# Three weight buffers at three places of a 128-byte frame, in a two-block transformer kernel

## The reference, cut to what matters

```
z = h @ w_in                                  # first block: mixer
merged = sum of gates[i] * (y_i @ w_branch[i]);  y = merged @ w_out
a, g = split(h @ w_up);  y = (gelu(conv(a)) * g) @ w_down
proj = x @ gla_w_in;     y = (o * silu(g)) @ gla_w_out      # GLA layer
kv = x @ w_kv; proj = x @ swa_w_in; y = (o * silu(g)) @ swa_w_out   # last layer
```

## Time and profile before

| | us |
|---|---|
| median of three runs | 746.49 |
| profiled execution, device time | 748.46 |
| its span, first to last instruction | 746.7 |
| PE busy | 721.3 |
| DVE busy | 522.7 |
| ACT busy | 395.9 |
| POOL busy | 106.3 |

### The profile page before, as it was taken

The page is one execution under the profiler, slowest core; times in us unless marked ns, Lnnn a source line. Parts: engine busy times, 40 slices in busy tenths (PEclk is TensorE's granted clock), DMA queues, the critical chain, the costliest instruction groups (busy, mean ns, idle before and its releaser), DMA issues.

```text
span 746.7 us, 14086 instructions
## 1 busy us (share of the span) xinstructions
PE 721.3 (97%) x5900; PEld 702.3 (94%) x5900; DVE 522.7 (70%) x763; ACT 395.9 (53%) x564; POOL 106.3 (14%) x90
## 2 busy tenths in 40 slices
PE   8899999998999999999999999999999999999995
PEld 6789899897898999999999989999999999999995
DVE  4879878876888777787777656936674456556665
ACT  4197454554364555445445347646555455556552
POOL 0040000000520200000001230000005265443000
PEclk9999999999999999999999999999999999999998
DMA  8995575566364355656565634534446544333101
GB/s 342 410 362 173 226 283 206 197 257 232 124 226 170 115 190 205 206 190 212 212 269 215 230 111 171 180 141 143 160 164 244 199 171 144 123 129 114 57 1 57
DMA packets 22265, 141.13 MB, mean 189 GB/s; under 512 B 2389, under 2 KB 3029, under 8 KB 6458
## 3 DMA queue, kind: packets, MB, share of 16 engines
q1 hardware_dynamic: 21626, 137.28, 50.7%
q0 software_dynamic: 576, 2.95, 1.0%
HBM read 139.17 MB, written 1.05 MB: 188 GB/s over the span
## 4 chain that ended last, share of the span: by engine, by line
PE 70%; DVE 12%; issue 6%; ACT 6%; DMA 4%; POOL 1%; SPq 0%; DVEq 0%; ACTq 0%
PE res L1593 20%; PE res L1594 20%; PE res L1595 20%; ACT wsplit L640 4%; DVE wsplit L1056 3%; DVE raw L1069 2%; PE pX L1796 2%; DMA shared<-in_w_ada 2%; DMA raw<-in_wts 1%; PE pS L1776 1%; DVE shared L1069 1%; DMA y<-in_w_ada 1%; ACT sq L655 1%; PE pS L1829 1%; PE pT L1786 1%
## 5 line engine op out<-in xcount | busy, mean ns | idle before, releaser
L1593 PE MATMUL res<-hs,wsplit 128*128 128x256 f32 (+1 forms) x1120 | 317.5, 283 | 3.2 <-DVE wsplit L1056 1.5
L1594 PE MATMUL res<-hs,wsplit 128*128 128x256 f32 (+1 forms) x1120 | 311.7, 278 | 0.0
L1595 PE MATMUL res<-hs,wsplit 128*128 128x256 f32 (+1 forms) x1120 | 311.5, 278 | 0.0
L1056 DVE TENSOR_TENSOR wsplit<-raw,wsplit 128x2048 fp32r<-128x2048 f32 (+3 forms) x101 | 226.7, 2248 | 117.7 <-ACT wsplit L640 108.1
L640 ACT ACTIVATE wsplit<-raw 128x2048 fp32r<-128x2048 f32 (+3 forms) x101 | 188.2, 1865 | 104.3 <-issue 74.5
L1593 PEld LDWEIGHTS res<-hs,wsplit 128*128 128x128 f32 (+1 forms) x1120 | 209.3, 187 | 4.7 <-issue 2.3
L1594 PEld LDWEIGHTS res<-hs,wsplit 128*128 128x128 f32 (+1 forms) x1120 | 209.3, 187 | 0.4
L1595 PEld LDWEIGHTS res<-hs,wsplit 128*128 128x128 f32 (+1 forms) x1120 | 209.0, 187 | 0.2
L538 POOL TENSOR_TENSOR sq<-sq,rope 128x512 f32<-128x512 f32 x18 | 39.5, 2195 | 78.3 <-ACT sq L655 78.3
L1595 PE MATMUL res<-us,wsplit 128*128 128x256 f32 x176 | 48.6, 276 | 0.0
L1593 PE MATMUL res<-us,wsplit 128*128 128x256 f32 x176 | 48.6, 276 | 0.0
(11 more groups left out here) (336 smaller groups left out, 1213.8 us busy)
## 6 DMA issues: line engine op xcount, KB each, us to landing
raw<-in_wts SPq DMA_DIRECT2D x97, 1024.0 KB, 5.0
raw<-in_w_ada SPq DMA_DIRECT2D x16, 1024.0 KB, 5.4
shared<-in_w_ada SPq DMA_DIRECT2D x6, 1024.0 KB, 11.9
gates<-in_wts SPq DMA_DIRECT2D x4, 768.0 KB, 13.3
raw<-in_wts SPq DMA_DIRECT2D x4, 768.0 KB, 5.3
y<-in_w_ada SPq DMA_DIRECT2D x2, 1024.0 KB, 9.3
x<-in_xT SPq DMA_DIRECT2D x2, 512.0 KB, 4.5
gv<-in_ln_rows POOLq DMA_DIRECT2D x1, 1024.0 KB, 7.6
```

Of the source, the lines that this page charges most:

```text
L1056: nc.vector.tensor_tensor(halves(c)[:, 1, 0:b], raw[RAW_OF["w", c] % RAW][:, 0:b], halves(c)[:, 0, 0:b].bitcast(f32), ALU.subtract).then_i ...
L1593: mm(out, a[:, 0, :], b[:, 0, :], start=first, stop=False)
L1594: mm(out, a[:, 1, :], b[:, 0, :], start=False, stop=False)
L1595: return mm(out, a[:, 0, :], b[:, 1, :], start=False, stop=last)
```

## The change

The three tiles `wsplit` lose their middle dimension and become 32 words longer. `halves` takes the two halves from word 0, 8 or 4 on, by the chunk's number modulo 3: byte 0, 32 or 16. Nothing else changes.

```diff
+SHIFT = (0, 8, 4)
...
-        wsplit = [sb(f"wsplit{i}", [P, 2, CW], f32r) for i in range(SPL)]
+        wsplit = [sb(f"wsplit{i}", [P, 2 * CW + 32], f32r) for i in range(SPL)]
...
-            return wsplit[c % SPL][:, :, :]
+            at = SHIFT[c % SPL]
+            return wsplit[c % SPL][:, at:at + 2 * CW].rearrange("p (e n) -> p e n", e=2)
```

## The result

The changed kernel takes 751.69 us (median of 19 runs, 750.70 to 754.14) against 747.33 us of the kernel before (19 runs beside it, 745.82 to 753.45): ratio 1.0043, 95% interval [1.0022, 1.0063]. The ratio is not the quotient of the medians: 13 of the 19 runs of the kernel before lie between 745.8 and 749.1 us (median 746.62) and six above 752. Against the 13 the change costs 5.1 us, by the means of all runs 3.2. The forecast was 752 us, with "within 1%" as the likeliest outcome (0.52). The number is right, and so is the mechanism in kind: the place of the operands sets the spacing, and the feed-forward part holds the cost. But the prediction counts the place by 128 bytes where the runs go by 256. Several of its terms are wrong by that, and that their errors cancel is luck.

The account below looks back on a forecast made before the run. The prediction took the start-to-start spacing of the `three` matmuls as the bound. Its terms, +3.9 (byte 32), +1.3 (byte 16) and 0 (byte 0), sum to +5.2 us on a median of 746.49, say 752 us; range 740 to 758.

Parts of the forecast that it names:

- The bound: Start-to-start spacing of the three matmuls of `three` sets most of the time; they hold all the chain in the feed-forward part.
- Every later tile keeps its place: Tiles grow to 16,512 bytes, 129 frames of 128 bytes, so every later tile moves by whole frames only.
- Slot 1, +2.9 us in FF: Feed-forward chunks with weights at byte 32: 528 matmuls go from 113.3 to 118.8 ns, +2.9 us.
- Slot 2, +1.3 us: Feed-forward chunks with weights at byte 16: midway between distances 64 and 32, 480 × 2.75 ns, +1.3 us.
- Slot 0, 0: Chunks with weights still at byte 0: distance stays 64, taken as 0, bounds +2.5 and −2.7 us.
- The rest of the sum, +1.0: Byte-32 chunks outside the feed-forward part: last layer +0.3, GLA layer +0.4, before 240 us +0.3.
- ACT and DVE, 0: The split into weight halves on ACT and DVE keeps its times; bounds 7 ns a chunk, 0.7 us overall, taken as 0.
- The place is no cause: Rival: order of work before a stretch sets the spacing everywhere, so nothing moves, 746.5 us; chance 0.17.
- The tight spacing dies: Rival: cutting the unbroken run at each chunk leaves byte-0 and byte-16 chunks wide too, +10.0 us, 756.5 us; chance 0.20.
- The tight spacing spreads: Rival: place jumps at chunk borders bring 113.3 ns everywhere, as `turned` does, −8.4 us, 738 us; chance 0.18.
- K: Experiments' theory at distance 64: a spacing lasts through PE's pauses until places or roles change; about 744 us for e9.
- R: Experiments' rival theory at distance 64: each pause of PE settles the spacing anew; 746 us for e9.

Follow-up runs that it names:

- e6: Kernel before with the three shifts 0, 32 and 16 bytes, unused pads keeping all later tiles in place modulo 256; 750.85 us, ratio 1.0001.
- e7: Kernel before with all three weight tiles 32 bytes further, everything else in place modulo 256; 752.07 us, ratio 1.0016.
- e8: Kernel before with all three weight tiles moved by 128 bytes and everything behind them by 256, nothing lengthened; 745.05 us, ratio 0.9934.
- e12: Changed kernel with its longer tiles, shifts set to 32, 0 and 32 words, so weights stand at distance 64 again; 750.14 us, ratio 1.0004.
- e9: Kernel before with one more call of `turned` (three matmuls, roles swapped) ahead of the last layer's first q chunk; 753.17 us, ratio 1.0043.
- e5: Changed kernel with all shifts set to 0, so only the 128 bytes of extra length per tile remain; 744.32 us, ratio 0.9898.
- e11: Changed kernel with all shifts set to 0, the same kernel as e5 run again; 744.50 us, ratio 0.9926.
- e10: Kernel of e5 with one more call of `turned` ahead of the last layer's first q chunk; 744.26 us, ratio 0.9932.

## Why the prediction came out right, step by step

- **The bound.** Right. The spacing of `three` sets the time, at an unchanged granted clock, and FF holds the cost, as the windows were to show: +4.5 us where "about 4" was forecast.
- **Every later tile keeps its place.** True modulo 128, wrong modulo 256, and the runs go by 256 (e6, e7, e8, e12). From this step come the next three errors. Five distances were in the trace before: 64, 160, 0 and 96 modulo 256, and 192 in the chunks with moving weights. The only two that are 128 apart, 64 and 192, both showed 113.3 as well as 117.8 ns there, so they did not tell 128 from 256.
- **Slot 1, +2.9 us in FF.** Mis-sized. The prediction took 118.8 ns from the earlier trace rows, which stand at 160 by the right count, while slot 1 stands at 32: 116.8 ns, 528 × 3.5 = +1.8 us.
- **Slot 2, +1.3 us.** Mis-sized the other way. It stands at 176, not between 32 and 64: 118.9 ns, at the upper bound given, 528 × 5.2 = +2.7 us. Slots 1 and 2 together: 4.2 forecast, 4.5 measured.
- **Slot 0, 0.** Right in FF (113.6 ns), but at distance 192 it did become tight in the last layer: 283 × (114.8 − 117.7) = −0.8 us, and in the GLA layer 180 × (115.2 − 117.8) = −0.5.
- **The rest of the sum, +1.0.** Wrong in sign. Behind FF the change is −0.2 us, by the starts of the stages +0.2 in the GLA layer, +0.4 in its output projection, −0.5 in the last layer and −0.3 in the last projection. In the GLA layer slot 0's gain stands against the products with moving weights (192 matmuls, from 113.3 to 115.7 ns before to 117.8 to 119.1, some +0.8), in the last layer against slot 2 (+0.3). Ahead of FF it is −1.1 us; this start lies between 239.9 and 241.7 us in the 14 profiles with no order by distance, so I put it down to no cause.
- **ACT and DVE, 0.** Right: 2292 and 1914 ns.
- **The sum.** +5.2 forecast; +3.1 between the two profiled executions, neither with the wide FF of e9, and +4.4 between the medians. The runs of the kernel before in its upper group raise that median, by 0.7 us over the lower group's, and the sum knew nothing of them. That 752 was met to 0.3 us is therefore luck; the direction and the place of the cost are not.
- **The place is no cause.** Fell: chunks that follow each other every 5.6 us differ by slot, over and over. The Trainium skill, "SBUF — State Buffer", section "Who interferes with whom", calls TensorE's two read ports independent and has TensorE wait on no one. The trace does not agree, if that is to mean that the place of its operands costs nothing: the three slots take 113.6, 116.8 and 118.9 ns in FF of the changed kernel. That the two reads hinder each other is an argument from these times; no run shows it directly.
- **The tight spacing dies.** Fell: slot 0 is tight between two dearer neighbours.
- **The tight spacing spreads.** Fell as told (slot 1 is not under 115 ns), yet its half on slot 0 came true, by the distance and not by the jump: e8, without a jump, has 114.2 to 114.7 ns in the last layer in all slots. `turned`, on which this rival and the term of slot 0 leaned, is no switch that can be relied on: e9 passes it and stays wide.

What stays open is what decides between 113.3 and 117.8 ns at distance 64 (and at 192, where wide pieces are rare in FF but one in four in the last layer). It differs between runs of one kernel, and the times that K and R gave were both missed. The 14 profiles together say when the spacing changes. I compare means of 12 intervals, in chunks with stationary weights at 64 or 192. Inside a chunk without a break it changes from tight to wide or back in none of 438, with a break in 53 of 309. From one chunk to the next it changes at 9 of 432 borders where PE runs on, and at 54 of 182 where over 0.2 us lie between the last start of one and the first of the next. Behind `turned`, ahead of the third chunks of `WOUT` and `UP`, it changes 14 of 18 times, nine of them from tight to wide. So the spacing holds, with few exceptions, while the row of matmuls is unbroken, which is nearer to R than to K, and a break can throw it either way; what decides at a break is not known.

## What to carry to other kernels

Where TensorE alone sets the time, take the distance between the starts of the moving and the stationary operand as a quantity of its own, and measure it: here 128 bytes more for each of three buffers, with no other edit, are worth 2.6 to 3.3 us behind the feed-forward part (e5, e11), and none of the 30 runs of e5, e10 and e11 lies near 753, while shifts of 16 and 32 bytes cost 2.9 and 2.2 in that part. A change of a buffer's length moves every tile behind it, so try the length alone beside the edit that needs it. And where the runs of a kernel fall into two groups, compare stages in the trace before a ratio of medians: e9's interval lies wholly above 1 with no change ahead of the stage that made it so.

## What the runs showed of the hardware that was not expected

Spacing of a 128 x 128 by 256 matmul with its weight load, at a granted clock of 1.00, by "moving minus stationary" modulo 256, median over chunks of the feed-forward part of all 14 profiles: 113.3 ns at 192 (157 chunks, 99% under 115), 113.3 at 64 (161 chunks, 77% under 115, the others at 117.8), 116.7 at 32 (76), 116.6 at 48 (11), 118.6 at 160 (21), 118.8 at 176 (22). From the kernel before come 120.0 at 0 and at 96. Distances 128 apart are not alike (32 and 160, 48 and 176), except 64 and 192 in their better spacing. All these have stationary weights. With moving weights distance 192 is no sure gain: of 33 such chunks in the GLA and the last layer 12 are under 115 ns, of 36 at 64 seven are.
